# Half products with sums on GpSimd, and roots through logarithms, in the RWKV pairs of a decoder step

## What is computed

```
h = rmsnorm(x, g_pre)
p_shift, q_mem, gate = split(h @ w_in)
s = p_shift + (prev - p_shift) * mu              # prev: the token before
r, k, v, wl, al = split(s)
w = -softplus(-(w0 + tanh(wl) @ w_w2)) - 0.5     # decay = exp(-exp(w))
a = sigmoid(a0 + al @ w_a2)
kk = k * k_k;  kk = kk / maximum(sqrt(sum(kk * kk)), 1e-12)      # per head of 64
k_mod = k * (1 + (a - 1) * k_a)
y, wkv = wkv_recurrence(r, decay, k_mod, v, kk, a, wkv0)
yn = (y - mean) * rsqrt(var + 64e-5) * ln_w + ln_b               # per head of 64
o = concat(yn + sum(r * k_mod * r_k) * v, memory attention) * silu(gate)
x = x + rmsnorm(o @ w_o, g_post)
```

## Time and profile before

| | |
|---|---|
| runs (3) | 1728.71 us median, 1726.29 to 1731.70 |
| profiled execution | 1735.68 us, span 1734.0 us |
| busy: PE, DVE, ACT, POOL | 94%, 61%, 23%, 9% of the span |
| chain that ended last | PE 76%, DVE 10%, ACT 5%, DMA 5%, issue 2% |
| turns -1 to 12 | from about 976 to 1526 us of the span |
| mean granted TensorE clock | 0.978 |

### The profile page before, as it was taken

The page is one execution under the profiler, slowest core; times in us unless marked ns, Lnnn a source line. Parts: engine busy times, 40 slices in busy tenths (PEclk is TensorE's granted clock), DMA queues, the critical chain, the costliest instruction groups (busy, mean ns, idle before and its releaser), DMA issues.

```text
span 1734.0 us, 27840 instructions
## 1 busy us (share of the span) xinstructions
PE 1627.5 (94%) x9596; PEld 1289.5 (74%) x9596; DVE 1058.9 (61%) x4997; ACT 392.2 (23%) x978; POOL 161.4 (9%) x295
## 2 busy tenths in 40 slices
PE   7999998899999999979989999999999999899995
PEld 6677776677777777658967777777777777788895
DVE  4786556646464555528862477777777777340755
ACT  2131111101121121220120333333333333221011
POOL 1121212112112212220000000000000000020000
PEclk9999999999999999999989999999999999999998
DMA  9699999999999999994452233333333323374431
GB/s 387 224 343 396 419 406 391 373 393 420 419 408 419 405 416 416 353 365 196 146 237 74 83 100 102 101 101 101 101 101 101 101 77 116 108 272 170 146 146 51
DMA packets 101726, 419.95 MB, mean 242 GB/s; under 512 B 41797, under 2 KB 46289, under 8 KB 91985
## 3 DMA queue, kind: packets, MB, share of 16 engines
q0 software_dynamic: 41680, 218.91, 31.9%
q1 hardware_dynamic: 53256, 187.54, 28.5%
q10 hardware_dynamic: 6648, 11.73, 1.8%
HBM read 405.28 MB, written 12.85 MB: 241 GB/s over the span
## 4 chain that ended last, share of the span: by engine, by line
PE 76%; DVE 10%; ACT 5%; DMA 5%; issue 2%; POOLq 0%; POOL 0%; SPq 0%; ACTq 0%; DVEq 0%
PE psum L733 25%; PE psum L1160 10%; PE psum L801 10%; PE psum L783 6%; PE psum L1023 5%; DMA kvr<-in_cv 3%; PE psum L722 3%; PE psum L771 2%; PE psum L1207 2%; DMA kvr<-in_ck 1%; PE psum L1217 1%; PE psum L759 1%; PE psum L744 1%; ACT gT L1759 1%; PE psum L824 1%
## 5 line engine op out<-in xcount | busy, mean ns | idle before, releaser
L1921 DVE CUSTOM_DVE_ANT_0 kvr<-kvr,arena 128x128 f32<-128x128 f32 x1488 | 323.5, 286 | 111.5 <-DMA kvr<-in_ck 111.4
L733 PE MATMUL psum<-hT,wring 128*128 128x264 f32 x1536 | 364.3, 394 | 0.0
L733 PEld LDWEIGHTS psum<-hT,wring 128*128 128x128 f32 x1536 | 291.1, 193 | 67.7 <-issue 19.6
L1160 PE MATMUL psum<-hT,kvr 128*128 128x264 f32 x1152 | 284.4, 392 | 1.8 <-DVE hT L2249 1.8
L1160 PEld LDWEIGHTS psum<-hT,kvr 128*128 128x128 f32 x1152 | 214.2, 192 | 42.8 <-issue 8.9
L783 PE MATMUL psum<-hT,kvr 128*128 128x264 f32 x512 | 121.4, 393 | 0.0
L1921 DVE DVE_READ_ACCUMULATOR2_ANT arena<- 128x1 f32 x1488 | 121.3, 82 | 0.0
L783 PEld LDWEIGHTS psum<-hT,kvr 128*128 128x128 f32 x512 | 97.5, 194 | 16.9 <-issue 0.4
L667 POOL DMA_DIRECT2D kvr<-in_cv x128 | 68.0, 531 | 379.4 <-PE psum L1023 302.8
L1023 PE MATMUL psum<-kvr,arena 128*32 128x384 f32 x1024 | 97.6, 497 | 4.8 <-DMA kvr<-in_cv 4.8
L667 POOL DMA_DIRECT2D kvr<-in_ck x128 | 67.9, 530 | 216.7 <-issue 216.0
(11 more groups left out here) (433 smaller groups left out, 2322.6 us busy)
## 6 DMA issues: line engine op xcount, KB each, us to landing
kvr<-in_ck POOLq DMA_DIRECT2D x128, 768.0 KB, 11.9
kvr<-in_cv POOLq DMA_DIRECT2D x128, 768.0 KB, 11.2
kvr<-in_wrkv SPq DMA_DIRECT2D x12, 3072.0 KB, 13.4
kvr<-in_wo SPq DMA_DIRECT2D x14, 2048.0 KB, 8.2
wring<-in_wkv SPq DMA_DIRECT2D x12, 2048.0 KB, 11.9
wring<-in_wm SPq DMA_DIRECT2D x8, 2048.0 KB, 12.7
wring<-in_wg SPq DMA_DIRECT2D x8, 2048.0 KB, 12.2
kvr<-in_wg SPq DMA_DIRECT2D x8, 2048.0 KB, 8.5
```

Of the source, the lines that this page charges most:

```text
L733: last = mm(psum[:, m % 2, 0:n], w[:, k, t * P:(t + 1) * P], rhs[:, k, 0:n], start=(k == 0), stop=(k == KT - 1))
L1160: last = mm(psum[:, m % 2, 0:T], w[:, k, t * P:(t + 1) * P], hT[:, k, :], start=(k == 0), stop=(k == KT - 1))
L1921: last = v_.tensor_tensor_reduce(page, page, qb[:, n % 2, h * P:(h + 1) * P], 1.0, 0.0, ALU.mult, ALU.add, S[:, n % 2, j * FH + h:j * FH + ...
```

## The change

The r and k tiles of pairs 1 to 11 are no longer 32 full products but 56 of 132 columns: with the contraction cut into halves of 1024 features, the two tiles as two column halves of the weights and the tokens as two halves of 132, seven products of half-size matrices (Q1 to Q7, eight steps of 128 features each) replace eight. They need sums of weights and of inputs. GpSimd makes the four sums of the inputs once (on `hT`, to the memory of `xT`; x is kept in DRAM meanwhile and brought back before the last residual), and four sums of 1024 columns for each pair's weights (`wsum1`, in the memory of `qT1`, and in place in `runit`). The seven results are joined on VectorE (`joined_pair`). Pair 0 and the v tiles stay as they are.

The inverse roots of the keys' square sums and of the variances were root on ScalarE and reciprocal on VectorE; now ScalarE takes the logarithm and then the exponential of -0.5 times it. The bound of 1e-12 becomes a minimum of the inverse with 1e12 in the multiplication by the key; the two squares move from VectorE to ScalarE, and `centred` moves up into `keys` on VectorE. `level(0)` on ScalarE moves ahead of the variances' function.

```diff
@@ SyncE
                 pair(j, "vrkv", vunit[:, j, :], f"v1_full{j}")
+            sp.wait_ge(sem("x_new"), 4)
+            sp.dma_start(xkept, xT[:, :, :].rearrange("p k t -> p (k t)")).then_inc(sem("x_in2"), 16)
             sp.wait_ge(sem("p_done"), M_LORA + 2)
...
                 blocks(o + 1)
+            sp.wait_ge(sem("p_done"), M_RKV + 3 * RP)
+            sp.dma_start(xT[:, :, :].rearrange("p k t -> p (k t)"), xkept).then_inc(sem("x_in2"), 16)
             for v in range(3, 16):
@@ GpSimd
+            pool.wait_ge(sem("x_in2"), 32)
+            pool.wait_ge(sem("h_out"), 16)
+            pt_(t1, b12, b11, ALU.subtract).then_inc(sem("t_sum"), 1)
+            pt_(t3, b22, b12, ALU.subtract).then_inc(sem("t_sum"), 1)
+            pool.wait_ge(sem("t_sum"), 4 + 1)
+            pt_(t2, b22, t1, ALU.subtract).then_inc(sem("t_sum"), 1)
+            pool.wait_ge(sem("t_sum"), 4 + 3)
+            pt_(t4, b21, t2, ALU.subtract).then_inc(sem("t_sum"), 1)
+            pool.wait_ge(sem("at_t"), 2 * MH + FH)
+            for u in range(1, RP):
+                m, at0, o = M_RKV + 3 * u, 4 * (FEW0 + u - 1), u - 2
+                a11, a12, a21, a22 = pair_weights(u % 2)
+                pool.wait_ge(sem(f"r_full{u % 2}"), 16 * (u // 2 + 1))
+                if u > 1:
+                    pool.wait_ge(sem("w_sum"), at0)
+                    pool.wait_ge(sem("p_done"), m - 1)
+                    pool.wait_ge(sem("prepared"), u - 1)
+                pt_(wsum1, fold(a21), fold(a22), ALU.add).then_inc(sem("w_sum"), 1)
+                pool.wait_ge(sem("w_sum"), at0 + 1)
+                if o >= 1:
+                    pool.wait_ge(sem("gn_ms"), o)
+                pt_(a21, a11, a21, ALU.subtract).then_inc(sem("w_sum"), 1)
+                pool.wait_ge(sem("p_done"), m + 1)
+                if o >= 0:
+                    pool.wait_ge(sem("tl_in"), o + 2)
+                pt_(wsum1, wsum1, fold(a11), ALU.subtract).then_inc(sem("w_sum"), 1)
+                pool.wait_ge(sem("w_sum"), at0 + 3)
+                if o >= 1:
+                    pool.wait_ge(sem("pair_done"), o)
+                pt_(fold(a12), fold(a12), wsum1, ALU.subtract).then_inc(sem("w_sum"), 1)
@@ TensorE: rows Q2, Q1, Q5, Q4, Q7, Q6, Q3 of 8, then 32 half rows of v, cut in 12 parts
+                    for at in range(CUT[n], CUT[n + 1]):
+                        q, k = ROWS[at]
+                        if at in (0, 24, 48):
+                            pe.wait_ge(sem("p_free"), m + at // 24 + 1)
...
+                        if k == 0:
+                            if q == Q5:
+                                pe.wait_ge(sem("t_sum"), 8)
+                                pe.wait_ge(sem("w_sum"), sums + 1)
+                            if q == Q7:
+                                pe.wait_ge(sem("w_sum"), sums + 2)
+                            if q == Q6:
+                                pe.wait_ge(sem("w_sum"), sums + 3)
+                            if q == Q3:
+                                pe.wait_ge(sem("w_sum"), sums + 4)
@@ ScalarE
+                def pair_projected(t):
...
+                    if t == 1:
...
+                        act.wait_ge(sem("y_out"), sums + 1)
+                        ac(pm[:, 1, :], pb[:, 1, 1:T + 1], ACT.Copy, scale=om[:, b, 1:2])
+                        ac(shout[:, 3 * (o + 2) + 1, :], pb[:, 1, NPR:T + 1], ACT.Copy)
+                        ac(pm[:, 0, 0:TH], pb[:, 0, 1:rest], ACT.Copy, scale=om[:, b, 0:1])
+                        return
+                    act.wait_ge(sem("p_done"), m + 3)
+                    act.wait_ge(sem("y_out"), sums + 2)
+                    v = psum[:, m % 2, TH:TH + T]
+                    ac(pb[:, 2, 1:T + 1], v, ACT.Copy)
+                    ac(shout[:, 3 * (o + 2) + 2, :], v[:, NPR - 1:T], ACT.Copy)
+                    ac(pm[:, 2, :], v, ACT.Copy, scale=om[:, b, 2:3])
+                    ac(pm[:, 0, TH:T], pb[:, 0, rest:T + 1], ACT.Copy, scale=om[:, b, 0:1])
+                    ac(shout[:, 3 * (o + 2), :], pb[:, 0, NPR:T + 1], ACT.Copy).then_inc(sem("p_free"), 1)
...
                     ac(aa, B[:, 0:T], ACT.Sigmoid, bias=vec(A0)).then_inc(sem("wa_out"), 1)
+                    act.wait_ge(sem("mix"), o + 2)
+                    ac(df, sx[:, 1, :], ACT.Square, scale=vec(K_K)).then_inc(sem("kk_sq"), 1)
+                if late:
+                    act.wait_ge(sem("gn_in"), 3 * (o - 1) + 2)
+                    ac(gdf, yT, ACT.Square).then_inc(sem("gn_in"), 1)
                 if prepare:
+                    act.wait_ge(sem("nm_zero"), 1)
                     act.wait_ge(sem("kk_ss"), o + 2)
-                    ac(kk, A[:, 0:T], ACT.Sqrt).then_inc(sem("kk_rt"), 1)
+                    ac(kk, A[:, 0:T], ACT.Ln, bias=tiny[:, 0:1]).then_inc(sem("kk_rt"), 1)
+                level(0)
                 if late:
                     act.wait_ge(sem("gn_ms"), o)
-                    ac(grn, grn, ACT.Sqrt).then_inc(sem("gn_rt"), 1)
-                level(0)
+                    ac(grn, grn, ACT.Ln).then_inc(sem("gn_rt"), 1)
+                if prepare:
+                    act.wait_ge(sem("kk_rt"), 2 * (o + 1) + 1)
+                    ac(kk, kk, ACT.Exp, scale=-0.5).then_inc(sem("kk_rt"), 1)
+                if late:
+                    act.wait_ge(sem("gn_rt"), 2 * (o - 1) + 1)
+                    ac(grn, grn, ACT.Exp, scale=-0.5).then_inc(sem("gn_rt"), 1)
@@ ScalarE: projected(1) now stands behind solution(1)
@@ VectorE
+                def joined_pair(part):
...
+                    dve.wait_ge(sem("p_done"), m + part + 1)
+                    if part == 0:
+                        ch.do(v_.tensor_copy(r1_, q(Q1)))
+                        v_.tensor_copy(k1_, q(Q5))
+                        tt(r0_, r1_, q(Q2), ALU.add).then_inc(sem("p_free"), 1)
+                    elif part == 1:
+                        ch.do(tt(r1_, r1_, q(Q6), ALU.add))
+                        ch.do(tt(k0_, r1_, q(Q7), ALU.add))
+                        ch.do(tt(r1_, r1_, k1_, ALU.add))
+                        ch.do(tt(k1_, k1_, k0_, ALU.add))
+                        ch.do(tt(k0_, k0_, q(Q4), ALU.add))
+                        dve.sem_inc(sem("p_free"), 1)
+                        dve.sem_inc(sem("y_out"), 1)
+                    else:
+                        tt(r1_, r1_, q(Q3), ALU.add).then_inc(sem("y_out"), 1)
...
                 def normal_keys():
-                    dve.wait_ge(sem("kk_rt"), o + 2)
-                    ch.do(ts(kk, kk, 1e-12, None, ALU.max))
-                    ch.do(v_.reciprocal(kk, kk))
-                    ch.do(tt(kk, kkr, kk, ALU.mult))
+                    dve.wait_ge(sem("kk_rt"), 2 * (o + 2))
+                    ch.do(stt(kk, kk, 1e12, kkr, ALU.min, ALU.mult))
...
                 def normed():
-                    dve.wait_ge(sem("gn_rt"), o)
-                    ch.do(v_.reciprocal(grn, grn))
+                    dve.wait_ge(sem("gn_rt"), 2 * o)
@@ VectorE: joined_pair(0) behind the first two products of the samples' state, (1) behind blocks, (2) behind prepared
```

More of the change, by code:

```diff
@@ L412, in trunk_step @@
         nm1, rsum1, rinv1 = (r1.take(2) for _ in range(3))
+        tiny = r1.take(1)
         rs1 = r1.take(T)
@@ L1744, in turn_of @@
                 solution(0)
-                projected(1)
+                if not -2 < o < RP - 2:
+                    projected(1)
                 right_side(1)
@@ L2291, in keys @@
                     ch.do(ts(kkr, k, col(K_K), None, ALU.mult))
-                    tt(df, kkr, kkr, ALU.mult).then_inc(sem("kk_sq"), 1)
+                    if late:
+                        centred()
                     dve.wait_ge(sem("wa_out"), o + 2)
@@ L2380, in turn_of @@
                     diagonals()
-                if late:
+                if late and not prepare:
                     centred()
@@ L2403, in turn_of @@
                     ch.do(tt(s3, s3, bs(lw), ALU.mult))
+                    joined_pair(0)
                     dve.wait_ge(sem("z_y"), 2 * (o + 1) + 1)
@@ L2413, in turn_of @@
                     blocks()
+                    joined_pair(1)
                     dve.wait_ge(sem("z_y"), 2 * (o + 1) + 2)
@@ L2416, in turn_of @@
                     v_.tensor_reduce(ys[:, a, :], x3(Z[:, 1, :]), AX.X, ALU.add).then_inc(sem("prepared"), 1)
+                    joined_pair(2)
                 else:
```

84 lines of the change are left out of this document (72 added, 12 removed).

## The result

The changed kernel takes 1739.99 us (median of 6 runs, 1738.07 to 1742.72) where the kernel before, beside it, takes 1730.2 (6 runs): a ratio of 1.0059, with a 95% interval of 1.0043 to 1.0074. It is slower by 0.6%, where 0.4% faster was forecast. The profiled execution has a span of 1740.0 us, 6.0 more than before, and a mean granted clock of 0.979 (0.978).

A forecast was written before the change was run, and what follows sets the result against it. TensorE's own work was taken to bound a turn, plus a 1.2 us gap. Terms -5.9 - 1.4 - 0.5 + 1.0 + 0.5 = -6.3 us gave 1722.4 us from a median of 1728.71; range 1708 to 1741.

The forecast's parts named there:

- TensorE's saving: r and k tiles as seven half products: 12.60 us for 14.24, 1.65 less in each of 11 turns.
- The joins costed at nothing: At a turn's end on VectorE, the second join's 1.65 us was to fit with 0.8 us of room left.
- That is at most 0.15 us a turn: In middle turns, the cost of GpSimd's sums meeting VectorE's shift products and key scaling.
- The early turns: Turn 0, turn -1 and the turn before, where sums have less cover: taken -0.5, +1.0 and +0.5 us.
- two whole sums waited for: Turn -1's upper end, +4.5 us: VectorE's key scaling and scaled keys wait for the third and fourth sum.
- The size of a sum: One GpSimd sum, with no row showing it: between 1.2 and 3.7 us, 2.4 taken.
- (a): Rival, chance 0.22: each VectorE operation with two inputs in the same memory waits for a whole GpSimd sum; +1.9 us, 1730.6.
- (c): Rival, chance 0.18: sums of 3 us or more, waited for at `normal_keys`; about +11 us, 1740.
- The roots: In middle turns, VectorE loses two reciprocals, 3.6 us, but ScalarE's chain brings the scaled keys 0.3 us later.
- (d): Rival, chance 0.09: one table serves logarithm and exponential, taking 1.3 us from ScalarE's chain in ten turns; -12 more, 1710.
- The transfers: Keeping x (2.2 MB) in DRAM and bringing it back cost nothing; exposed, each some 6 us once.
- Turns 10 and 11: Without half products, moving `level(0)` and the squares shortens TensorE's waits, sigmoids come 0.75 late: -1.4 us for both.

The follow-up runs named there:

- roots alone: The kernel before with only logarithm and exponential for root and reciprocal, both squares on ScalarE and `level(0)` moved; no half products, sums or joins: ratio 0.9961.
- no joins: The changed kernel with all 48 GpSimd sums over 8 columns and VectorE's nine join operations left out, against the kernel before: ratio 0.9910.
- the last kernel above: The changed kernel with half products only from pair 3, input sums behind turn -1, second join ahead of the block solve, mask copies early: 0.9917 to the kernel before.
- the join ahead: The changed kernel with VectorE's second join moved from behind the block solve to ahead of it: ratio 1.0031 to the kernel before.
- short sums: The changed kernel with all 48 GpSimd sums over 8 columns instead of 1024 or 1056: ratio 0.9995 to the kernel before.
- the masks: The changed kernel with ScalarE's six mask copies moved from the turn's end to behind `solution(0)`: ratio 1.0047 to the kernel before.
- both moves made: The changed kernel, half products from pair 1, with second join ahead of the block solve and mask copies behind the solution: ratio 1.0003 to the kernel before.
- the second join late: The changed kernel with the second join moved behind `prepared`'s signal: ratio 1.0235 to the kernel before.
- the first sum short: The changed kernel with only the first of each pair's four weight sums over 8 columns instead of 1024: ratio 1.0025 to the kernel before.
- the half products alone: The changed kernel with root and reciprocal put back and squares on VectorE; half products, sums and joins stay: ratio 1.0150 to the kernel before.

## Why the prediction was wrong

By parts, over turns -1 to 9, from the differences between the runs' traces: the roots -6.1 (roots alone less before), the half products without sums and joins -8.1 more (no joins less roots alone), the joins +10.6, the sums +11.4. That is +7.8. Turn -2 adds 4.0. The forecast had -5.4 in those eleven turns and +0.5 in turn -2, so it missed by 13.2 and 3.5 us. Each part holds some of the clock, by one profiled execution of each kernel: at most -1.7, -1.7, +1.7 and +3.4 us. By place: turns 1 to 9 are +1.1 for -5.9 forecast, the three turns ahead of them +10.7 for +1.0, turns 10 and 11 -0.3 for -1.4.

*TensorE's saving* was right. From the start of each record to the next one's, idle time left out, the 96 records of full products in a turn took 22.04 us before; the 112 of half products and 32 of full ones take 20.57 in the last kernel above: 1.48 less, 1.65 forecast. A half product in a row is 1.57 us for 14 records, 0.112 each. It moves the turn's end by 0.68 (41.96 with the roots alone, 41.28 without joins); the rest becomes waits for VectorE and ScalarE, as the prediction had it in kind.

*The joins costed at nothing* is the step that failed in turns 1 to 9, where they cost 7.8 us: "I find 0.8 us of room left there" for the second join. In the turn of the earlier trace rows VectorE ended 3.2 us ahead of TensorE's next turn. In the change it ends 0.4 to 0.6 ahead where the small transfers land as they do in that turn. They don't always. VectorE's wait for them, in the kernel before, turn by turn:

```profile
1083.80 0.16 DVE L2342 TENSOR_TENSOR kmT<-kmT 32x14 f32<-32x14 f32 x1 [0.54 <-DMA kmT<-near]
...
1213.90 0.16 DVE L2342 TENSOR_TENSOR kmT<-kmT 32x14 f32<-32x14 f32 x1 [1.42 <-DMA kmT<-near]
...
1257.26 0.16 DVE L2342 TENSOR_TENSOR kmT<-kmT 32x14 f32<-32x14 f32 x1 [2.16 <-DMA kmT<-near]
```

Those two turns are the ones of 43.95 and 43.24 us. The late transfer made only the second of them longer, where TensorE waited 0.35 us for the small solve; the first is long mostly by its clock. The row was there; I had read one middle turn and multiplied it by nine. With 1.65 us of join behind the same wait, four turns in nine were long (waits of 2.65, 1.71, 2.43 and 2.24 us), and with the join ahead, where the transfers were as late (6.4 and 6.5 us from the first issue out to the issue back in turns 2 and 6, for 4.7 to 5.5 in the others), those turns took 42.7 and 42.8 in place of 44.0 and 43.6. The other share, 0.5 to 0.7 us where the transfers are on time, comes over ScalarE. The forecast had its sigmoids 0.75 us later and found that eaten by the lost squares; but TensorE waits 1.0 to 1.3 us for L1849 in the change, where 0.5 was forecast; with short sums it waits 0.69 us in turn 1 with the joins and 0.15 without, and with the second join ahead, moving the masks takes that wait away.

Why the transfers are late can be read in the traces, down to what lies beside them. In the stretch from the first issue out to the issue back, the change's turn 2 (1126.04 to 1132.72) has a packet of another queue, the one that the page calls "instruction" (80 such packets in the span, 1.31 MB); turn 4 (1213.88 to 1218.57) has none:

```profile
q8 instruction: 1, 0.02, 0.9%
```

Of the 204 round trips in the 17 traces, 63 took over 5.2 us, and in 61 of these stretches lies such a packet of 16384 bytes, of 0.9 to 1.5 us; of the other 141, it lies in 2. In the kernel before it is turns -1, 4 and 5, in the change turns 2, 3, 6 and 7. So how often VectorE's chain is late goes with where the packets of this queue fall. There are 76 of them in the span before and 80 after; that the change's additional instructions moved them is my guess from the queue's name, and no run shows it. That the packet holds up the small ones is argued from this; no run moved one of them apart.

*"That is at most 0.15 us a turn"* for the meetings is the second step that failed: 0.54 in the change (4.9 in nine turns). I had put the first sum on the shift products, 1.4 us ahead of the sigmoids, and overlooked what stands ahead of those. It is the samples' state: L2589, 8 columns, stands ahead of L2593, L2593 ahead of a transfer on ScalarE's queue, that ahead of the table load. With both moves made the sums cost 0.7 us in all of turns 1 to 9, as the prediction had it for a chain with room.

*The early turns* missed more than the nine others, 9.7 us. Turn -1 was given -3.5 to +4.5, taken +1.0: it is +4.3 (41.67 for 37.34). Turn 0: -1.6 to +0.6, taken -0.5: +2.4, out of its bounds; the joins weren't in them (0.9), and the roots alone already make it 1.8 longer (41.95 for 40.12), which is the clock: TensorE is busy for 41.50 us there for 39.85, with 3.41 us at the lower level for none. Together the first three turns are +10.7 by the trace, for +1.0 forecast. Turn -2: 0 to +3.0, taken +0.5: +4.0, above its bounds too. In two other runs with the same four input sums (the second join late, the first sum short) the clock stays at 1.00 in it and it takes 32.44 us: 2.3 are waits, 1.7 the lower clock. The bounds had no term for more time at the lower clock. VectorE's rows in turn -1 show the price whole, twice in a row:

```profile
983.14 2.12 DVE L2478 SCALAR_TENSOR_TENSOR arena<-arena 128x264 f32<-128x264 f32 x1 [1.89 <-ACT arena L1863]
985.30 0.43 DVE L2480 TENSOR_TENSOR oT<-psum,arena 128x264 f32<-128x264 f32 x1
985.65 2.11 DVE L2481 TENSOR_TENSOR arena<-arena 128x264 f32<-128x264 f32 x1
```

Here the upper ends of the bounds, which I had worked out for "two whole sums waited for", were nearly the value or below it: a bound whose two ends stand for two mechanisms has no middle.

*The size of a sum*, 2.4 us taken between 1.2 and 3.7, is 2.36 (11 each of L748, L752, L756 and L760), 2.42 to 2.46 for the inputs. Of the rivals, (a) was right in its mechanism, every meeting a whole sum, and short by 9.4 us in its sum (1730.6); (c) has the right time, 1740, by luck: its length of sum isn't there. *The roots* and the third load came as written, and (d), one load fewer, did not: three loads of 1.28 us a turn, the one at L1863 between the logarithm and the exponential, and the gap of L2360 gone; the eleven turns gained 6.1 with nothing else changed. *The transfers* of x: no wait for them stands in the trace. *Turns 10 and 11* were given -1.4 and gave -0.3 (-0.7 and +0.4).

What stays open: when TensorE is granted the lower clock. Each kernel has it in turn -1, at or behind the wait for the scaled keys (2.25 us before, 5.61 in the change, which has more of it), but with a wait of 2.39 us in both, the last kernel above had 3.41 us of it in one execution and 6.83 in the other, and the half products alone have it in middle turns too.

## What to carry to other kernels

Read the wait that the moved work will stand behind in every turn, not in one: a chain end with 0.8 us of room and a transfer that is at times 2 us late has none. Read the granted clock of each turn before a longer turn is put down to a wait. Place sums on a second engine by which operations of the other one they meet, and what stands behind those; here, one join moved into a wait that exists anyway and one block of copies moved up a queue gave 0.6%, and full products in the turns that fill the pipeline 0.6 to 0.9%. And an edit that gives nothing alone (the masks) is to be tried again behind the one that takes the wait ahead of it away.

## What the hardware showed

While GpSimd sums 1024 columns in SBUF (2.36 us), VectorE's operations with two inputs in SBUF waited for its end (L2478 went from 0.43 to 2.12 us, L2532 from 0.49 to 1.75), an 8-column copy inside SBUF too (L2589, from 0.16 to between 1.39 and 2.33), and with an input in PSUM they didn't (the copy L2587 kept its 0.29, L2439 its 1.21). A reciprocal of 2 columns in SBUF (L1966), which began twice within a sum of the inputs, kept its 0.17 us. ScalarE's operations beside the first sum kept their lengths (0.39, 0.48 and 0.41 us from 1101.10 on, and the same with short sums). The same 32 KB over DRAM and back took 4.7 to 4.9 us from the first issue out to the issue back in most turns and 5.3 to 6.7 in others, and 61 of these 63 had a 16 KB packet of the instruction queue beside them.
